# A hybrid diffusion step on one core: both filter orders, the conditioning rows and the loads of the opening stretch put in another order

## The chip, the cores and the metric

The kernel runs on one core of a Trainium2 chip. The metric is the device time of one execution in microseconds (us), lower is better. All numbers are f32.

## The reference, cut to what matters

The reference is one step of a two-layer network over 128 prompt tokens and 256 latent tokens, width 1024. Layer 0 mixes tokens with a Hyena long convolution and with grouped attention, layer 1 with latent attention; each is followed by a mixture of experts. The change touches only what comes before and inside the Hyena part of layer 0:

```python
def modulation(cond, l):
    return jax.nn.silu(cond) @ w_mod[l] + b_mod[l]          # shift, scale, gate: 6 x 1024

h = jnp.sin(fr * (z @ w1 + b1))                             # _hyena_spectrum(n, ...)
h = jnp.sin(fr * (h @ w2 + b2))
h = (h @ w3 + b3).reshape(n, HY_ORDER, 2, HY_DIM)           # 2 orders, forward and backward, 512 channels
h = h * jnp.exp(-t01[:, None] * deltas[None, :])[:, None, None, :]
h_fwd, h_bwd = h[:, :, 0], h[:, :, 1]
filt2n = jnp.concatenate([h_fwd, zeros, h_bwd[:0:-1]], axis=0)
filt2n = filt2n * lax.rsqrt(jnp.sum(filt2n * filt2n, axis=0, keepdims=True) + EPS)
return jnp.fft.rfft(filt2n, axis=0)

def _hyena(u, conv_w, conv_b, spec, bias):
    v, x1, x2 = jnp.split(_short_conv3(u, conv_w, conv_b), 3, axis=-1)
    z = x1 * long_conv(v, spec[:, 0], bias[0])              # irfft(rfft(v) * spec) + bias * v
    z = x2 * long_conv(z, spec[:, 1], bias[1])
```

The input of that mixer is `_rmsnorm(x) * (1 + sc1) + sh1`, times a 1024 x 2304 matrix (`ev_w_in`): 1536 columns for the Hyena part, 768 for queries, keys and values.

## The kernel before

Each engine has a program written out by hand, and semaphores join them. There is no scheduler: an engine does its work in the order in which it is written. Tokens stand in three tiles of 128 (`t` = 0 the prompt, 1 and 2 the latent tokens).

**Weights.** SyncE (SP) sends 1 MB pieces through a ring of nine slots (`send`); TensorE reports a slot as used (`piece_used`). The first eight pieces are the shift and scale columns of layer 0 (the stage "start": four chunks of 512 columns, two pieces each), the next nine are `ev_w_in`. Between them SP loads the filter weights `w3`, the table `decay`, the bias `hybias` (broadcast to 128 rows, twice 256 KB) and the tokens `x`. GpSimd (POOL) loads small constants, and the DFT tables `dftp` and `dfts` after piece 3.

**Conditioning.** `mod_product` multiplies a chunk by the two condition vectors in 32-column products, ScalarE copies the row out (`mod_row`), stores it in HBM (`mod_rows`), and POOL loads it back transposed (`move_row`). VectorE sums and adds it (`mod_add`); then shift `modT` and scale `modA` are ready.

**Filters.** `hidden` has 64 rows and a row of ones. `filters(od)` makes, for three token tiles and both directions, the taps of order `od`: a 65-row product on TensorE, times `decay` on VectorE, then sum and difference of the directions on VectorE. ScalarE squares them, `energies(od)` sums the squares over the rows by products with ones, and `spectrum(od)` multiplies sum and difference by the DFT tables. VectorE divides by the energy and adds the bias.

**Order on TensorE.** Two small products and two sines; chunks 0 and 1 between them; `filters(0)`; chunks 2 and 3; `energies(0)`; 24 transposes of the normed tokens (`mixer_turn`); a wait for the modulated tokens; `spectrum(0)`; then `ev_w_in` in nine pieces, numbers 6, 7, 8, 0, ..., 5. `filters(1)` stands ahead of piece 7, `energies(1)` and `spectrum(1)` ahead of piece 8. After the last piece come the transposes of the convolved channels and the DFTs of the tokens. I call the nine pieces' products *the projections*. Every f32 product is two instructions in the trace.

## Time and profile before

| | |
|---|---|
| median of three runs | 930.47 us (928.52 to 930.5) |
| the profiled execution | 928.82 us, of which the span is 927.0 |
| TensorE busy | 803.5 us (87%) |
| VectorE, ScalarE, GpSimd busy | 379.2, 272.2, 108.1 us |
| moved by DMA | 220.19 MB, mean 238 GB/s |

TensorE works through nearly the whole span, so what it does, and what it waits for, is the time to look at. The opening stretch, up to about 190 us of the span, is the one that the change touches. In rows of the trace "x12" counts instructions, and a busy time that covers several runs from the first start to the last end.

### The profile page before, as it was taken

Reading aid. Unit: us, or ns where it says so; the run is one execution under the profiler, and the core shown is the slowest. Engines: PE = TensorE matmul, PEld = TensorE weight load, DVE = VectorE, ACT = ScalarE, POOL = GpSimd, SP = SyncE. Lnnn points to the kernel's source line nnn. Section 1 sums busy time; section 2 is a strip of 40 time slices with the busy share of each in tenths; the row PEclk is TensorE's granted clock in tenths of the full one; section 3 lists DMA queues with packets and bytes.
Section 4 is the critical chain, followed back from the end, with each engine's and each line's share of the span. In section 5 each row is a group of like instructions: output and inputs, shape, how many; then the busy total and the mean of one; then the engine's idle time right before and its main releaser. Section 6 shows DMA issues by size and latency. Waiting matters only on the chain.

```text
span 927.0 us, 11593 instructions
## 1 busy us (share of the span) xinstructions
PE 803.5 (87%) x4091; PEld 447.8 (48%) x4091; DVE 379.2 (41%) x848; ACT 272.2 (29%) x636; POOL 108.1 (12%) x157
## 2 busy tenths in 40 slices
PE   4779999999888996999988599888899978999860
PEld 0236665544443464555536346545554555555430
DVE  3366583265064243332212644664651432322114
ACT  1241212121451042222211536565540332222111
POOL 2300000001000003101013002212200022010120
PEclk9989999999978997899999799999989998999995
DMA  9991222259991347899997966202109388999975
GB/s 275 370 341 50 71 93 95 90 172 345 258 371 53 130 134 250 315 405 410 411 387 262 347 246 246 93 1 93 48 1 346 125 288 312 396 411 410 384 257 208
DMA packets 84561, 220.19 MB, mean 238 GB/s; under 512 B 9636, under 2 KB 19549, under 8 KB 84185
## 3 DMA queue, kind: packets, MB, share of 16 engines
q1 hardware_dynamic: 73570, 197.04, 58.9%
q0 software_dynamic: 9120, 18.75, 5.9%
q10 hardware_dynamic: 1816, 3.68, 1.1%
q8 instruction: 33, 0.54, 0.2%
q14 instruction: 22, 0.18, 0.1%
HBM read 214.77 MB, written 14.89 MB: 248 GB/s over the span
## 4 chain that ended last, share of the span: by engine, by line
PE 63%; DMA 15%; DVE 8%; ACT 4%; SPq 3%; issue 3%; DVEq 1%; POOLq 1%; POOL 0%; ACTq 0%
PE ps L923 57%; PE ps L930 4%; DMA arena<-in_moe_w_up_dram 3%; DMA ring<-in_w_mod_dram 2%; DMA h_rows<-xn 2%; PE ps L1150 2%; DMA ring<-in_moe_w_down_dram 2%; DMA xn<-y_rows 2%; SPq L643 1%; DVEq L1909 1%; DVE negmax L1962 1%; SPq L660 1%; DMA hT<-h_rows,rows_in 1%; SPq L690 1%; ACT hT L1626 1%
## 5 line engine op out<-in xcount | busy, mean ns | idle before, releaser
L923 PE MATMUL ps<-arena 128*64 128x256 f32 (+12 forms) x1164 | 237.6, 449 | 24.8 <-ACT hT L1626 5.9
L923 PEld LDWEIGHTS ps<-arena 128*64 128x64 f32 (+4 forms) x1164 | 128.6, 168 | 115.9 <-issue 71.9
L923 PE MATMUL ps<-ring,hT 128*128 128x512 f32 (+2 forms) x384 | 133.6, 507 | 4.5 <-issue 3.9
L923 PE MATMUL ps<-ring,arena 128*64 128x256 f32 (+1 forms) x784 | 111.3, 431 | 5.5 <-DMA ring<-in_moe_w_down_dram 4.2
L923 PEld LDWEIGHTS ps<-ring,hT 128*128 128x128 f32 x384 | 73.0, 192 | 62.9 <-issue 58.5
L923 PEld LDWEIGHTS ps<-ring,arena 128*64 128x64 f32 x784 | 53.9, 137 | 51.3 <-issue 28.3
L930 PE MATMUL ps<-ident,arena 128*128 128x128 f32 (+2 forms) x332 | 51.0, 293 | 17.2 <-DVE hT L1968 4.6
L1582 ACT ACTIVATE arena<-ps 128x256 f32<-128x256 f32 (+4 forms) x88 | 38.5, 454 | 85.9 <-PE ps L923 82.2
L923 PE MATMUL ps<-hT,ring 128*128 128x384 f32 x192 | 62.1, 486 | 0.0
L2294 DVE TENSOR_TENSOR arena<-arena,ps 128x128 f32<-128x128 f32 x37 | 10.6, 288 | 124.1 <-ACT arena L1688 124.1
L923 PE MATMUL ps<-ring,condT 128*32 128x512 f32 x384 | 52.7, 674 | 8.6 <-DMA ring<-in_w_mod_dram 7.9
L930 PEld LDWEIGHTS ps<-ident,arena 128*128 128x128 f32 (+2 forms) x332 | 39.4, 143 | 38.2 <-issue 15.8
L923 PEld LDWEIGHTS ps<-hT,ring 128*128 128x128 f32 x192 | 36.5, 190 | 25.2
L2297 DVE COPY arena<-ps 64x512 f32<-64x512 f32 x37 | 25.7, 694 | 42.6 <-PE ps L923 42.2
L1694 ACT ACTIVATE arena<-ps 64x512 f32<-64x512 f32 x37 | 21.8, 590 | 66.6 <-PE ps L923 61.7
L831 POOL DMA_INDIRECT y_rows<-arena,rows_in x16 | 16.0, 1001 | 166.3 <-DVE arena L2297 166.3
L923 PE MATMUL ps<-xn,arena 128*64 128x256 f32 (+2 forms) x144 | 32.8, 473 | 2.6 <-DVE hT L1990 2.4
L1688 ACT ACTIVATE arena<-ps 128x128 f32<-128x128 f32 x37 | 10.3, 278 | 81.9 <-PE ps L923 81.9
L1962 DVE TENSOR_REDUCE negmax<-ps 128x1 f32<-128x384 f32 (+1 forms) x48 | 20.8, 461 | 29.0 <-PE ps L923 28.5
L1643 ACT ACTIVATE arena<-ps,negmax 128x384 f32<-128x384 f32 (+1 forms) x48 | 24.1, 507 | 26.0 <-DVE negmax L1962 25.9
L1618 ACT ACTIVATE xn<-x 128x1024 f32<-128x1024 f32 x12 | 12.7, 1054 | 60.7 <-DVE x L2114 57.2
L923 PEld LDWEIGHTS ps<-ring,condT 128*32 128x32 f32 x384 | 10.6, 115 | 40.8 <-issue 27.4
(301 smaller groups left out, 871.7 us busy)
## 6 DMA issues: line engine op xcount, KB each, us to landing
ring<-in_w_mod_dram SPq DMA_DIRECT2D x48, 1024.0 KB, 9.4
ring<-in_moe_w_down_dram SPq DMA_DIRECT2D x22, 1024.0 KB, 16.8
ring<-in_moe_w_gate_dram SPq DMA_DIRECT2D x38, 512.0 KB, 12.9
ring<-in_moe_w_up_dram SPq DMA_DIRECT2D x38, 512.0 KB, 15.5
arena<-in_moe_w_gate_dram SPq DMA_DIRECT2D x36, 512.0 KB, 9.5
arena<-in_moe_w_up_dram SPq DMA_DIRECT2D x36, 512.0 KB, 10.9
arena<-in_moe_w_down_dram SPq DMA_DIRECT2D x15, 1024.0 KB, 13.7
ring<-in_ev_w_in_dram SPq DMA_DIRECT2D x9, 1024.0 KB, 13.3
```

The source lines that it names most:

```text
L831: pool.indirect_dma_start(y_rows, bass.IndirectOffsetOnAxis(ap=rows_in[:, NPAIR + c:NPAIR + c + 1], axis=0), ysb[:, c % 2, :], None, bound ...
L923: mm = pe.matmul(out, lhsT, rhs, **kw)
L930: mm = pe.transpose(out, src, ident[:, :])
L1150: mm = pe.transpose(ps[XT_BANKS[half]][:, q * P:(q + 1) * P], src[:, (4 * half + q) * P:(4 * half + q + 1) * P], ident[:, :])
L1582: drain_inc(act.activation(dst, src, kw.pop("func", ACT.Copy), **kw), stage, i)
L1618: act.activation(xn[:, t, :], x[:, t, :], ACT.Square, accum_out=ssq[:, s, t:t + 1]).then_inc(squares, 1)
L1643: drain_inc(act.activation(mprobs[:, i % 2, r, 0:nk], bank_of(f"mS{g}", u)[:, 0:nk], ACT.Exp, bias=negmax[:, c:c + 1], accum_out=psumexp[: ...
L1688: act.activation(sil[:, e % 2, :], ps[GU_BANKS[e % 2]][:, 0:P], ACT.Silu).then_inc(silu_ready[l], 1)
L1694: act.activation(dst, ps[Y_BANKS[e % 2]][0:HALF, :], ACT.Copy).then_inc(done[l], 1)
L1962: dve.tensor_reduce(negmax[:, c:c + 1], bank[:, 0:nk], AXX, ALU.max, negate=True).then_inc(negmax_ready, 1)
L2294: dve.tensor_tensor(mid[:, e % 2, :], sil[:, e % 2, :], ps[GU_BANKS[e % 2]][:, P:2 * P], ALU.mult).then_inc(mid_ready[l], 1)
L2297: dve.tensor_copy(dst, ps[Y_BANKS[e % 2]][HALF:P, :]).then_inc(y_read[1][l], 1)
```

## The change

1. SP loads the filter inputs first (they were on ScalarE's queue), then the condition vectors. `hybias` is 4 KB, no broadcast. The DFT tables go from POOL's queue to SP's, ahead of piece 4. Most small constants of POOL wait for piece 5.
2. The filter weights are padded: rows 65 to 127 of `w3` and `hidden` are zero, and products have 128 rows. GpSimd forms the sum and the half difference of the forward and backward weights once (`wsum`, `w3`), so TensorE gives sum and difference directly.
3. `filters`, `energies` and `spectrum` of both orders stand ahead of the projections. The energy division leaves the spectrum: the root of the energy is turned (`root_turn`), inverted, and folded into the short convolution's coefficients (`conv_scaled`); the bias becomes an addition to the first tap (`bias_taps`).
4. The four "start" rows are not stored and loaded back: eight 2-column products turn each (`mod_turn`).
5. 10 and 8 products of ones with ones (`warm`) stand ahead of the first two products. Energies are 32 rows wide instead of 128.

```diff
     B.stage("filt1", 1)
+    B.stage("filt2", 1)
     mod_stage("start", 0)
-    B.stage("filt2", 1)
+    B.stage("filt3.0", 2 * NT)
+    B.stage("modT0", 1)
+    B.stage("filt3.1", 2 * NT)
     mod_stage("start", 1)
...
+                    load(sp, in_filt, zT, d["zT"])
+                    load(sp, in_filt, filtc[0:EMB, 3 + HID:3 + 2 * HID], d["ev_filt_w1"][0])
...
                 if i == 2:
+                    sp.wait_ge(w3_ready, 1)
                     load(sp, in_filt3, w3[0:HID, :, :], d["ev_filt_w3"][0].rearrange("k (a b) -> k a b", b=HY))
                     load(sp, in_filt3, w3[HID:HID + 1, :, :], d["ev_filt_b3"].rearrange("k (a b) -> k a b", b=HY))
+                    load(sp, in_filt3, decay, d["decay"].rearrange("p (a b) -> p a b", b=HY))
+                    load(sp, in_filt3, hybias[0:1, :, :], d["ev_hy_bias"])
                 if i == 4:
...
+                    load(sp, in_spec, dftp, d["dft_p"].rearrange("p (a b) -> p a b", b=NPR))
+                    load(sp, in_spec, dfts, d["dft_s"].rearrange("p (a b c) -> p a b c", b=2, c=NSA))
...
+            loaded(pool, in_filt3)
+            pool.tensor_tensor(wsum, w3[:, 0::2, :], w3[:, 1::2, :], ALU.add)
+            pool.drain()
+            pool.tensor_tensor(w3[:, 1::2, :], w3[:, 0::2, :], w3[:, 1::2, :], ALU.subtract)
+            pool.drain().then_inc(w3_ready, 1)
...
-            for i in range(len(CHUNKS["start"])):
-                move_row("start", i)
...
+            def mod_turn(i):
+                l, v, half = CHUNKS["start"][i]
+                row = modrow_of("start", i)
+                bank = claim(f"modT{i}")
+                drained_wait(pe, f"mod{l}.{v}.{half}")
+                for j in range(KT):
+                    mm = product(bank[64 * half:64 * half + 64, 2 * j:2 * j + 2], row[:, j::KT], rowsel[:, :, 0], carries=False, start=True, stop=True)
+                fill_inc(mm, f"modT{i}")
...
+                        split = w3[:, 2 * od + 1, :] if r else wsum[:, od, :]
+                        mm = product(bank[:, :], hidden[:, t * P:(t + 1) * P], split, carries=False, start=True, stop=True)
...
+                for t, r in ((0, 0), (1, 0), (0, 1), (1, 1), (2, 0), (2, 1)):
+                    pe.wait_ge(esq_ready, od * (NT + 1) + max(t, 1) + 2)
+                    g = GRP[t]
+                    mm = product(bank[32 * g:32 * g + 32, :], onesm[:, 0:32], sqs[:, t, r, :], start=t < 2 and r == 0, stop=t != 1 and r == 1)
...
             for q in (6, 7, 8, 0, 1, 2, 3, 4, 5):
-                if q == 7:
-                    filters(1)
-                if q == 8:
-                    energies(1)
-                    spectrum(1)
-                if q == 0:
-                    pe.wait_ge(spec_done, 12)
...
             def filter_squares(od, t):
-                act.wait_ge(sum_ready, od * NT + t + 1)
+                act.wait_ge(tile_ready, od * NT + t + 1)
                 if od:
-                    filled_wait(act, "energy0", min(t, 1))
-                act.activation(filt[:, t, 0, :], sqd, ACT.Copy)
-                act.activation(sqs[:, t, 0, :], sqd, ACT.Square)
-                act.activation(sqs[:, t, 1, :], filt[:, t, 1, :], ACT.Square)
+                    filled_wait(act, "energy0")
+                for r in range(2):
+                    act.activation(sqs[:, t, r, :], filt[od][:, t, r, :], ACT.Square)
                 act.drain().then_inc(esq_ready, 1)
```

TensorE in the opening stretch, before: from `filters(0)` to the first piece of the queries, `filters(1)`, and the last of the 65-row products. "ring,condT" are conditioning chunks, "arena,gb" energies, "ident,xn" the transposes of the normed tokens, "ring,hT" projections of a piece.

```order
L923 MATMUL ps<-arena 128x512 x6
L923 MATMUL ps<-ring,condT 32x512 x16
L923 MATMUL ps<-arena,gb 128x512 x6
L930 MATMUL ps<-ident,xn 128x128 x24
L923 MATMUL ps<-arena 128x512 x10
L1366 MATMUL ps<-ident,arena 128x48
L923 MATMUL ps<-ring,hT 128x256 x24
L923 MATMUL ps<-arena 128x512 x6
L923 MATMUL ps<-ring,hT 128x256 x24
L923 MATMUL ps<-arena,gb 128x512 x6
L923 MATMUL ps<-arena 128x512 x10
L923 MATMUL ps<-ring,hT 128x256 x24
```

And in the change, from `energies(1)` on ("rowsel" marks `mod_turn`, 128x32 the turned roots):

```order
L949 MATMUL ps<-arena,gb 32x512 x6
L949 MATMUL ps<-rowsel,modrow 64x2 x8
L1385 MATMUL ps<-ident,arena 128x32 x8
L949 MATMUL ps<-ring,condT 32x512 x8
L1422 MATMUL ps<-ident,arena 128x48
L949 MATMUL ps<-rowsel,hT 64x2 x8
L956 MATMUL ps<-ident,xn 128x128 x24
L949 MATMUL ps<-arena 128x512 x5
L1385 MATMUL ps<-ident,arena 128x32 x8
L949 MATMUL ps<-arena 128x512 x10
L949 MATMUL ps<-ring,hT 128x256 x72
L949 MATMUL ps<-hT,ring 128x384 x96
```

The 22 filter products that stood between the projections' first pieces are gone from there, and 15 of the 20 spectrum products stand between the turned tokens and the projections.

ScalarE, before, from the third chunk's row to the modulation (L1618 and L1620 are the norm of the tokens, L1582 the copy of a row, L1626 the modulation):

```order
L1582 ACTIVATE modrow<-ps 128x512
L1609 DMA mod_rows<-modrow 8x512
L1790 ACTIVATE arena<-gb 128x512
L1791 ACTIVATE arena<-gb 128x512
L1792 ACTIVATE arena<-arena 128x512
L1582 ACTIVATE hT<-ps 128x512
L1609 DMA mod_rows<-hT 8x512
L1618 ACTIVATE xn,ssq<-x 128x1024
L1620 ACT_TABLE_LOAD
L1620 ACTIVATE ssq<-ssq 128x1
```

The same stretch in the change (L1857 is the root of an energy, L1851 the squares, L1672 and L1674 the norm, L1634 the copies):

```order
L1857 ACT_TABLE_LOAD
L1857 ACTIVATE arena<-ps,gb 32x512 x2
L1851 ACTIVATE arena<-arena 128x512 x6
L1634 ACTIVATE modrow<-ps 128x512
L1672 ACTIVATE xn,ssq<-x 128x1024
L1674 ACTIVATE ssq<-ssq 128x1
...
L1634 ACTIVATE hT<-ps 128x512
L1857 ACTIVATE arena<-ps,gb 32x512 x2
L1680 ACTIVATE hT<-ps,modT,modA 128x128 x12
```

The squares of order 1 now stand behind the roots of order 0, and the copy of the last chunk's row stands behind the norm of all three token tiles, where it stood ahead of it.

## Rows read from the trace of the kernel before

**Rows 1.** The page: the span and the instructions.

```profile
span 927.0 us, 11593 instructions
```

**Rows 2.** The chain that ended last, 0 to 220 us: start, duration, what.

```profile
24.32 20.73 DMA ring<-in_w_mod_dram
...
45.10 1.98 PE ps L923 x8
...
47.81 5.30 DMA mod_rows<-hT
...
53.40 6.24 DMA hT<-mod_rows
...
185.74 2.62 PE ps L930 x24
```

**Rows 3.** Windows: busy us of each engine, granted clock, DMA share, GB/s.

```profile
25.00:45.00 20.00, 15.55 (x36) 4.15 (x34) 8.82 (x14) 5.60 (x10) 5.81 (x11) 1.00 1.04 370
```

**Rows 4.** TensorE in order of time, 52 to 130 us: start, duration, what.

```profile
62.41 11.06 PE L923 MATMUL ps<-arena 128*128 128x512 f32 x20 [5.92 <-ACT hT L1626]
...
73.59 10.63 PE L923 MATMUL ps<-ring,hT 128*128 128x256 f32 x48
84.05 5.32 PE L923 MATMUL ps<-arena 65*128 65x512 f32 x12
89.20 10.52 PE L923 MATMUL ps<-ring,hT 128*128 128x256 f32 x48
99.57 5.31 PE L923 MATMUL ps<-arena,gb 128*128 128x512 f32 x12
104.72 8.75 PE L923 MATMUL ps<-arena 128*128 128x512 f32 x20
113.30 10.52 PE L923 MATMUL ps<-ring,hT 128*128 128x256 f32 x48
123.66 6.61 PE L923 MATMUL ps<-hT,ring 128*128 128x384 f32 x20
```

**Rows 5.** TensorE in order of time, 0 to 60 us.

```profile
13.36 1.94 PE L923 MATMUL ps<-ring,condT 128*32 128x512 f32 x8 [0.90 <-DMA ring<-in_w_mod_dram]
...
18.54 1.94 PE L923 MATMUL ps<-ring,condT 128*32 128x512 f32 x8 [1.74 <-DMA ring<-in_w_mod_dram]
...
24.43 10.61 PE L923 MATMUL ps<-arena 65*128 65x512 f32 x12 [1.32 <-DMA gb<-in_ev_hy_bias_dram]
...
46.96 6.84 PE L923 MATMUL ps<-arena,gb 128*128 128x512 f32 x12
53.63 2.85 PE L930 MATMUL ps<-ident,xn 128*128 128x128 f32 x24
```

**Rows 6.** Windows of TensorE alone: busy, granted clock, DMA share, GB/s.

```profile
24.40:35.10 10.70, 10.67 (x16) 1.00 1.06 359
...
62.40:66.80 4.40, 4.39 (x5) 0.50 1.11 349
```

**Rows 7.** All engines, 0 to 70 us: loads issued at the start.

```profile
0.73 0.62 ACTq L643 DMA_DIRECT2D arena<-in_zT_dram  x1
...
1.67 0.98 SPq L660 DMA_DIRECT2D ring<-in_w_mod_dram  x2
```

**Rows 8.** GpSimd by line and shape.

```profile
L889 POOL TENSOR_TENSOR arena<-arena,statA 128x1152 f32<-128x1152 f32 x4 | 8.5, 2114 | 79.8 <-DVE statA L2069 79.8
```

**Rows 9.** TensorE, 196 to 260 us: conditioning chunks later on.

```profile
197.30 3.64 PE L923 MATMUL ps<-ring,condT 128*32 128x512 f32 x32
```

**Rows 10.** TensorE, 326 to 345 us: products of 16 columns.

```profile
337.00 1.86 PE L923 MATMUL ps<-routw,hT 128*128 128x16 f32 x16
```

**Rows 11.** ScalarE by line and shape, 0 to 70 us.

```profile
L1618 ACT ACTIVATE xn<-x 128x1024 f32<-128x1024 f32 x3 | 3.1, 1046 | 0.6 <-ACT hT L1582 0.6
...
L1791 ACT ACTIVATE arena<-gb 128x512 f32<-128x512 f32 x3 | 1.8, 613 | 0.0
...
L1620 ACT ACT_TABLE_LOAD x1 | 1.3, 1283 | 0.0
```

More of the change, by code:

```diff
@@ L80 @@
 }
-MOVED = [chunk for where in CHUNKS for chunk in CHUNKS[where] if chunk[1] not in (G1, G2)]
+MOVED = [chunk for where in CHUNKS if where != "start" for chunk in CHUNKS[where] if chunk[1] not in (G1, G2)]
 MODA_ORDER = [(0, 0), (0, 1), (1, 0), (1, 1)]
@@ L1342, in _, with warm @@
+            def warm(bank, n):
+                for _ in range(n):
+                    pe.matmul(bank[:, 0:P], onesm, onesm, start=True, stop=True)
+            pe.wait_ge(ones_set, 1)
+            bank = claim("filt1")
+            warm(bank, WARM_FIRST)
             loaded(pe, in_filt)
-            bank = claim("filt1")
             mm = product(bank[0:HID, 0:T], filtc[0:EMB, 3 + HID:3 + 2 * HID], zT, start=True, stop=True)
             fill_inc(mm, "filt1")
-            mod_step("start", 0)
+            bank = claim("filt2")
@@ L1347, in _ @@
+            warm(bank, WARM_SIN)
             loaded(pe, in_filt2)
             pe.wait_ge(sin_done, 1)
[L1349 removed]
             mm = product(bank[0:HID, 0:T], filtc[:, 3:3 + HID], hidden[0:HID, :], carries=False, start=True, stop=True)
             fill_inc(mm, "filt2")
[L1352 to L1358 removed]
@@ L1359, in _ @@
-            energies(0)
-            loaded(pe, in_mod)
-            for t in range(NT):
-                mixer_turn(0, t)
+            mod_step("start", 0)
+            pe.wait_ge(w3_ready, 2)
+            pe.wait_ge(sin_done, 2)
+            filters(0)
+            mod_turn(0)
+            filters(1)
+            mod_step("start", 1)
+            loaded(pe, in_spec)
+            spectrum(0, 1)
+            energies(0)
+            mod_turn(1)
+            mod_step("start", 2)
+            energies(1)
@@ L1363, in _ @@
+            mod_turn(2)
+            root_turn(0)
+            mod_step("start", 3)
             loaded(pe, in_dft)
-            spectrum(0)
             bank = claim("convT")
@@ L1367, in _ @@
             fill_inc(mm, "convT")
+            mod_turn(3)
+            for t in range(NT):
+                mixer_turn(0, t)
+            spectrum(1, 1)
+            root_turn(1)
+            spectrum(0, 0)
+            spectrum(1, 0)
             for i in range(6):
@@ L1600, in mod_row @@
                         act.wait_ge(mod_out[sent % 2], 16 * (sent // 2 + 1))
-                    if v in (G1, G2):
+                    if where == "start" and i >= 2:
+                        filled_wait(act, f"modT{i - 2}")
+                    if where == "start" or v in (G1, G2):
                         copy_out(name, 0, row, bank_of(name)[:, :])
@@ L1802, in heads_copy @@
                     copy_out(f"qkv{q}", t, qkv[:, t, q * 256:(q + 1) * 256], bank_of(f"qkv{q}", t)[:, 0:256])
+            mod_step("start", 0)
+            first_rows(0)
             for t in range(NT):
                 filter_squares(0, t)
-                if t:
-                    mod_step("start", t + 1)
+            first_rows(1)
+            mod_step("start", 1)
+            energy_roots(0)
+            for t in range(NT):
+                filter_squares(1, t)
+            mod_step("start", 2)
             loaded(act, in_x)
@@ L1920, in mod_step @@
                 rows = slice(64 * half, 64 * half + 64)
-                total = (moved_rows[where][:, 128:144] if where == "start" else row_total)[rows].rearrange("p (j c) -> p j c", c=2)
+                total = row_total[rows].rearrange("p (j c) -> p j c", c=2)
                 dve.wait_ge(mod_moved[n % 2], 16 * (n // 2 + 1))
@@ L1926, in mod_step, with mod_add, mod_scale @@
                 dve.tensor_tensor(modT[rows, l, v, :, :], total, modT[rows, l, v, :, :], ALU.add)
+                mod_scale(l, v, half)
+            def mod_add(i):
+                l, v, half = CHUNKS["start"][i]
+                rows = slice(64 * half, 64 * half + 64)
+                bank = filled_wait(dve, f"modT{i}")
+                turned = bank[rows, 0:2 * KT].rearrange("p (j c) -> p j c", c=2)
+                drain_inc(dve.tensor_tensor(modT[rows, l, v, :, :], turned, modT[rows, l, v, :, :], ALU.add), f"modT{i}")
+                mod_scale(l, v, half)
+            def mod_scale(l, v, half):
                 if half == 0 or v in (SH1, SH2):
@@ L2444, in _ @@
+            filters(0)
+            mod_add(0)
+            filters(1)
+            imaginary_copies(0)
+            bias_taps(0)
+            mod_add(1)
+            mod_add(2)
+            root_inverse(0)
             norm(0)
-            energies(0)
-            for i in range(1, 5):
-                mod_step("start", i)
+            bank = filled_wait(dve, "convT")
+            drain_inc(dve.tensor_copy(convT[:, :, :], bank[:, 0:48].rearrange("p (a b) -> p a b", b=3 * NCH)), "convT")
+            mod_add(3)
```

252 lines of the change are left out of this document (137 added, 115 removed).

## The prediction

> **What bounds the kernel now.** I began with the page and the chain of work that ended last, then read TensorE in order of time. The span is 927.0 us [rows 1]. On the chain, a weight piece is the first long entry: it lands at 45.1, TensorE multiplies it for 2.0 us, and then the row goes out to HBM (5.3) and comes back (6.2) [rows 2]. TensorE meanwhile runs out of work: 5.92 us idle, and it starts the first spectrum only at 62.41, once the tokens are modulated [rows 4]. From there to 185.74, where the transposes behind the projections begin [rows 2], it has no gap that a row shows. In this second part a microsecond of TensorE's work is a microsecond of the span; in the first part it is DMA that sets the pace: its share is 1.04 and it moves 370 GB/s from 25 to 45 us [rows 3], while a filter's products wait for a load before they start at 24.43 [rows 5].
>
> The projections themselves take, start to next start, 10.46 (73.59 to 84.05), 10.37 (89.20 to 99.57), 10.36 (113.30 to 123.66) and 62.08 us (123.66 to 185.74): 93.3 us [rows 2, 4]. Were nothing else between them, they would have to start at 185.74 - 93.3 = 92.5 us for the end that they have now. The other 30 us from 62.4 on are `spectrum(0)` 11.2 (with a small transpose), `filters(1)` 5.15, `energies(1)` 5.15 and `spectrum(1)` 8.6 [rows 4]. So the question of this change is one number: when do the projections start, if all of the filter work is ahead of them? Call it S. The gain is 92.5 - S. What follows the projections is the same work, and its loads are released by it: ring slots by pieces used, the first expert weights by the second inverse DFT. I let all of it move as one block.
>
> **TensorE's clock.** The same 128x512 instruction takes two lengths. 12 of them from 84.05 take 5.15 us, 0.43 each [rows 4]; 12 from 24.43 take 10.6, 0.88 each [rows 5]. From 62.4 to 66.8, five take 4.39, again 0.88, and the granted clock there is 0.50, that is 1.2 instead of 2.4 GHz [rows 6]. At 24.4 the column says 1.00 [rows 6]; there I go by the length, and call it slow too. The slow filter products had 65 rows and stayed slow for all of 10.6 us; the 128-row energies from 46.96 take 6.84 for 12, which is slow ones for about 3 us and fast ones after; the spectra from 62.41 turned fast after 4.4 us [rows 5, 6]. The padded products have 128 rows. I take it that the first 4 of them are slow and what follows is fast.
>
> **When the filters start.** Four more small loads stand ahead of the first weight pieces on SP. The longest of them is issued in 0.62 us, and the pieces' issue began at 1.67 [rows 7], so the delay is up to 2.5 us; DMA begins with little in its queues, so I take 1.5. TensorE took up the second piece at 13.36 and the third at 18.54, with 1.5 MB (`w3` and a piece) between them: 5.2 us [rows 5]. Now `w3` and `decay`, 1.25 MB, come right after the second: 13.4 + 1.5 + 4.3 = 19.2. Then GpSimd adds and subtracts 1024 columns each. The nearest row is 2.11 us for 1152 columns [rows 8]: 1.9 each, 3.8 in all. The filters start at 23, where they now start at 24.4; the two sines are done by then, and the `warm` products are hidden behind the same wait. The Trainium skill (GPSIMD Engine Reference, 3.1 on elementwise work) speaks against giving this work to GpSimd: it gives 4.5 us for 2048 columns where VectorE takes half. By it the filters would start 0.7 us later, an estimate from that page; no run here has shown this very operation.
>
> **TensorE's work from there to S.** `filters(0)`: 4 slow and 8 fast instructions, 3.5 + 3.4 = 7.0. `filters(1)`: 5.2. Four half spectra of 10 instructions: 17.2. Three conditioning chunks: two take 3.64 when fast [rows 9], so 1.8 each, 5.5. That row also shows that 32-column products at different columns run side by side: 32 instructions at 0.11 each, a quarter of 0.43. The new energies are 32 wide in two places: 8 instructions pairwise and 4 alone, 8 x 0.43 = 3.5 each, 7.0 for both, where they took 5.2 each. `mod_turn`: the nearest row is 16 instructions of 16 columns in 1.7 us (337.00 to the next start; 1.86 with the tail) [rows 10]; its weights are half as wide, so 0.8 is the other end. I take 1.3, four times 5.2. Two `root_turn`s of 8 transposes at 0.12 each (24 take 2.85 [rows 5]): 1.9. The 24 transposes of the tokens 2.8, the convolution's 0.2. Sum: 52.0 us.
>
> **Stalls in it.** Two, both by ScalarE's order. (a) The squares of order 1 stand behind the root of order 0. The first energy ends at about 45.3; then a table load of 1.28, two roots and six squares of 0.61 each [rows 11], with drains: the last squares are ready at 51.5, those that `energies(1)` needs first at 50.3. TensorE, after a turn and a chunk (3.1), is there at 48.5. It loses 1.8. (b) The last chunk's row is copied only after the norm of all three tiles, and VectorE takes up the norm only after the turned roots, at 56.5. Three squares of 1.05 [rows 11] in turn with small steps of VectorE take 4 us or so, then 0.6 for the copy: 60.9. TensorE is there at 58.4: 2.5 us lost. Behind that nothing is late: the half spectrum of order 1 covers the modulation (12 instructions each on ScalarE and VectorE), and the remaining ones cover its copies. Together 4.3, and 0.5 for banks.
>
> S = 23 + 52.0 + 4.8 = 79.8, and the gain 92.5 - 79.8 = 12.7 us. Against the profiled execution's 928.8 us that is 916.1. The median of the runs, 930.5, stands 1.7 above that execution; I put the changed kernel's median between, at **917 us**.
>
> **What costs nothing, and its cover.** The removed store and reload (11.5 us with the sums behind them) are worth nothing beyond this sum: they are on the path before, but S is set by TensorE's work. DMA: the eight conditioning pieces, filters, tables and tokens are 12 MB, at 370 GB/s [rows 3] some 34 us, so the last chunk is there well ahead of 56; all of `ev_w_in` by about 66, ahead of S. If that cover were gone, each us late is a us. The small constants that POOL now loads after piece 5 (six ahead of the convolution's transpose, at some 0.6 of issue each as `zT` [rows 7]) land around 47, some 10 us early. The two scaled copies per channel tile on ScalarE add under 0.7 us to a tile that TensorE takes 62.08 / 12 = 5.2 us for.
>
> **Rivals.**
> *The zero rows do not count* (0.13). The padded filter products stay at 0.88, as the 65-row ones did. For it: 10.6 us of slow products that nothing sped up. Against: the instruction now names 128 rows, and those did speed up. Then 20 instructions cost 0.45 more, 9 us: S near 88.8, 925 to 926 us.
> *TensorE's order is tighter than I count* (0.15). `mod_turn` at 0.8, the clock already fast when the filters start, weights there 2 us earlier and no stall (b): 2 + 1.8 + 2 + 2.5 = 8 us less: 908.
> *The clock never holds in the opening* (0.06). This one ends slower. Chunks, turns of 2 columns and short waits come between all the wide products, and if they let the clock fall, the 48 us that I count as fast take up to twice as long. It decides at 12.7 us: if more than a quarter of that work runs slow, the gain is gone; if all of it does, S is 128 and the kernel at 960; half of it gives 940. Before, a chunk between wide products at 197.3 stays fast [rows 9], which speaks against. The Trainium skill (TensorE: Matmul & The Clock Gate, Part 4 on transposes) says that transposes do not count as busy for the clock; by it the 24 token transposes behind stall (b) would let it fall, and the half spectrum after them would run slow for its 10 instructions, some 4 us by the two lengths. In the rows, 24 transposes from 53.63 end with the fall, but a wait of 5.92 us stands between [rows 4, 5], so they don't decide it.
> *Nothing gained* (0.02): the opening ends where it did, because a load (`in_dft` or `x`) takes the place of the old wait at some 12 us later than I have it.
>
> **How the numbers follow.** My forecast, 911 to 922, has 0.64. With the tighter order to 908 and the zero-row case to 925 the range is 907 to 925, and leaves out the clock that never holds. A measurement of this kernel can tell about 0.2%, 1.9 us, from no change. Faster: all of the first three but the edge, 0.91; same 0.02; slower 0.07, which is the third rival and a load that I have not seen.
>
> **What would show it.** Filters start at 22 to 25 us, and their instructions fall from 0.88 to 0.43 within the first five; the second energies wait 2 us for ScalarE squares; `mod_turn` of the last chunk waits 2 to 3 us for the row's copy; the first "ring,hT" product starts at 77 to 83 and the transposes behind the projections 93 us later; from there to the end the two traces keep one distance. Wrong would be: the weights' sum on GpSimd taking twice its row, a granted clock of 0.50 between 45 and 80 us, or a distance that shrinks once the expert weights bind.

## The result, and the profile after

The changed kernel took 924.44 us (median of 20 runs, 916.4 to 930.17), the kernel before 929.31 us (20 runs in turn with it, 923.75 to 937.78). The ratio is 0.994, with a 95% interval of 0.9914 to 0.9967: faster by about 5.6 us, not by 12.7. (The two medians stand 4.9 us apart; the ratio is taken over the runs in the fast state alone, and one of the 20, at 930.17, was not in it.) The time is inside the range given, at its upper edge, and outside the narrower forecast of 911 to 922.

The profiled execution of after took 929.42 us, longer than its own median. So I read stages by where they stand in the span, not by the span.

```profile
span 927.6 us, 11800 instructions
...
PE 815.1 (88%) x4207; PEld 464.2 (50%) x4207; DVE 354.3 (38%) x822; ACT 278.6 (30%) x648; POOL 111.1 (12%) x155
```

TensorE is busy for 11.6 us more than before (work and slower clock together: the mean granted clock of this trace is 0.929, before's 0.947) and VectorE for 25 us less. TensorE in order of time, the opening (start, duration, what, and in brackets the idle time before it and who ended it):

```profile
23.05 7.98 PE L949 MATMUL ps<-arena 128*128 128x512 f32 x12 [6.81 <-POOLq L796]
30.96 2.08 PE L949 MATMUL ps<-rowsel,modrow 128*64 128x2 f32 x16
32.97 5.42 PE L949 MATMUL ps<-arena 128*128 128x512 f32 x12
38.31 1.92 PE L949 MATMUL ps<-ring,condT 128*32 128x512 f32 x16
40.17 4.56 PE L949 MATMUL ps<-arena 128*128 128x512 f32 x10
44.66 3.63 PE L949 MATMUL ps<-arena,gb 128*32 128x512 f32 x12
48.22 2.08 PE L949 MATMUL ps<-rowsel,hT 128*64 128x2 f32 x16
50.23 1.92 PE L949 MATMUL ps<-ring,condT 128*32 128x512 f32 x16
52.48 3.63 PE L949 MATMUL ps<-arena,gb 128*32 128x512 f32 x12 [0.33 <-ACTq L1852]
56.04 2.08 PE L949 MATMUL ps<-rowsel,modrow 128*64 128x2 f32 x16
58.05 0.68 PE L1385 MATMUL ps<-ident,arena 32*128 32x32 f32 x8
58.66 3.41 PE L949 MATMUL ps<-ring,condT 128*32 128x512 f32 x16
...
62.92 2.05 PE L949 MATMUL ps<-rowsel,hT 128*64 128x2 f32 x16 [0.58 <-ACT hT L1634]
64.90 4.57 PE L956 MATMUL ps<-ident,xn 128*128 128x128 f32 x24
69.31 4.46 PE L949 MATMUL ps<-arena 128*128 128x512 f32 x10
...
82.99 31.24 PE L949 MATMUL ps<-ring,hT 128*128 128x256 f32 x144
...
175.99 2.78 PE L956 MATMUL ps<-ident,arena 128*128 128x128 f32 x24
```

Most rows have their counterpart in [rows 4, 5]. Filters start at 23.05, where 24.43 stood, behind a wait of 6.81 us for GpSimd; the wait of 5.92 us for the tokens is gone; the projections start at 83.0, where 92.5 was their equivalent before; the transposes behind them stand at 175.99, 9.6 us ahead of before's, which this view puts at 185.58 (the 185.74 of [rows 2] is the chain's figure; the chain of after has 176.15). The rows with 128x2 are the turned conditioning rows, 2.0 us for 16.

Now the same view further on, where the change touches only the list of stages, and adds one wait of VectorE for copies of the spectra that were made long before:

```profile
203.63 8.85 PE L949 MATMUL ps<-xn,arena 128*128 128x512 f32 x20
215.27 5.34 PE L949 MATMUL ps<-ring,condT 128*32 128x512 f32 x32 [2.78 <-DVE arena L2606]
221.49 8.93 PE L949 MATMUL ps<-arena 128*128 128x128 f32 x48 [0.89 <-ACT arena L1634]
```

and the same piece of before, with the transposes behind the projections as its first row:

```profile
185.58 2.78 PE L930 MATMUL ps<-ident,arena 128*128 128x128 f32 x24
...
213.22 8.85 PE L923 MATMUL ps<-xn,arena 128*128 128x512 f32 x20
222.01 3.64 PE L923 MATMUL ps<-ring,condT 128*32 128x512 f32 x32
226.23 8.96 PE L923 MATMUL ps<-arena 128*128 128x128 f32 x48 [0.59 <-DVE arena L2512]
```

Up to 203.63 after leads by 9.6 us. Then it waits 2.78 us for VectorE, the conditioning chunk takes 5.34 us instead of 3.64, and at the second inverse DFT the lead is 226.23 - 221.49 = 4.7 us. Half of what the opening won is given back here. VectorE's row for that moment shows the releaser, an instruction that reads a PSUM bank and ends at 215.2:

```profile
214.53 0.68 DVE L2606 TENSOR_TENSOR arena<-ps,arena 128x512 f32<-128x512 f32 x1
```

**Who meets whom.** The eight PSUM banks are given out by one list. A stage without banks of its own takes the next ones in turn:

```python
    def stage(self, name, count, banks=None):
        out = []
        for i in range(count):
            if banks is None:
                b = self.turn
                self.turn = (self.turn + 1) % 8
```

The chunks of the later conditioning (`mod_stage("gqa", i, BANK_M)`) have fixed banks, 6 and 7 by turns. The change adds four turned rows and two root turns to the list, takes two energy results off it, and so moves `self.turn` by 4 for all that follows. Worked out from the list, the second forward DFT (`fwd1`, six results) had banks 5, 6, 7, 0, 1, 2 and now has 1, 2, 3, 4, 5, 6. The chunk behind it takes bank 6. Before, that was the second of six results, long read; now it is the last, and the chunk waits until VectorE's product at L2606 has read it. This was a theory (A) until the first two experiments.

### The profile page after: what moved, and what is told of

It reads as the page before. It is cut to its first block, busy times and chain, and to the rows that moved or that the text cites. A ratio compares the mean times of both kernels' runs of the same rounds, so it can differ in the third digit from the quotient of the medians.

```text
span 927.6 us, 11800 instructions
## 1 busy us (share of the span) xinstructions
PE 815.1 (88%) x4207; PEld 464.2 (50%) x4207; DVE 354.3 (38%) x822; ACT 278.6 (30%) x648; POOL 111.1 (12%) x155
## 4 chain that ended last, share of the span: by engine, by line
PE 69%; DMA 10%; DVE 7%; ACT 4%; issue 4%; DVEq 1%; SPq 1%; POOLq 1%; ACTq 0%; POOL 0%
PE ps L949 61%; DMA arena<-in_moe_w_up_dram 5%; PE ps L956 5%; PE ps L1186 2%; DVEq L1983 1%; DMA h_rows<-xn 1%; DMA xn<-y_rows 1%; DMA hT<-h_rows,rows_in 1%; SPq L703 1%; DMA hT<-h_rows,row_now 1%; DVE xn L2445 1%; DVE negmax L2047 1%; DMA mod_rows<-modrow 1%; PE ps L1200 1%; ACT arena L1634 1%
## 5 line engine op out<-in xcount | busy, mean ns | idle before, releaser
L949 PE MATMUL ps<-arena 128*64 128x256 f32 (+11 forms) x1164 | 236.6, 448 | 23.6 <-POOLq L796 6.8
L949 PEld LDWEIGHTS ps<-arena 128*64 128x64 f32 (+3 forms) x1164 | 128.5, 168 | 112.8 <-issue 65.2
L1634 ACT ACTIVATE arena<-ps 128x256 f32<-128x256 f32 (+4 forms) x94 | 42.2, 463 | 89.2 <-PE ps L949 85.6
L2379 DVE TENSOR_TENSOR arena<-arena,ps 128x128 f32<-128x128 f32 x37 | 10.7, 288 | 124.8 <-ACT arena L1742 124.8
L949 PE MATMUL ps<-ring,condT 128*32 128x512 f32 x384 | 50.3, 655 | 2.8 <-DVE arena L2606 2.8
L1742 ACT ACTIVATE arena<-ps 128x128 f32<-128x128 f32 x37 | 10.2, 277 | 82.3 <-PE ps L949 82.3
L1672 ACT ACTIVATE xn<-x 128x1024 f32<-128x1024 f32 x12 | 12.7, 1055 | 60.1 <-DVE x L2199 57.2
L1186 PE MATMUL ps<-ident,hT 128*128 128x128 f32 x136 | 20.0, 294 | 11.5 <-DMA hT<-h_rows,rows_in 8.6
```

Source lines behind the costliest of these rows:

```text
L949: mm = pe.matmul(out, lhsT, rhs, **kw)
L1186: mm = pe.transpose(ps[XT_BANKS[half]][:, q * P:(q + 1) * P], src[:, (4 * half + q) * P:(4 * half + q + 1) * P], ident[:, :])
L1634: drain_inc(act.activation(dst, src, kw.pop("func", ACT.Copy), **kw), stage, i)
L1672: act.activation(xn[:, t, :], x[:, t, :], ACT.Square, accum_out=ssq[:, s, t:t + 1]).then_inc(squares, 1)
L1742: act.activation(sil[:, e % 2, :], ps[GU_BANKS[e % 2]][:, 0:P], ACT.Silu).then_inc(silu_ready[l], 1)
L2379: dve.tensor_tensor(mid[:, e % 2, :], sil[:, e % 2, :], ps[GU_BANKS[e % 2]][:, P:2 * P], ALU.mult).then_inc(mid_ready[l], 1)
```

## The experiments

All in five rounds beside the kernel before. The table sets two measures side by side: how far the second inverse DFT stands ahead of before's 226.23 in the one profiled execution, and what the whole kernel gained (one minus the ratio, of 930 us; the interval is the ratio's). One profile is one execution: with the same loads, the filters start anywhere from 22.09 (e4) to 23.61 (e5) in these traces, so I read no difference of less than about 1.5 us in one start alone as an effect, and go by rows next to each other.

```
                     median    ratio [95%]              ahead at the   whole kernel
                     us                                 inverse DFT    gained, us
after                924.44    0.994  [0.9914, 0.9967]      4.7          5.6
e1_banks             917.57    0.9876 [0.9841, 0.9911]      9.1         11.5
e2_clash             932.78    1.0035 [1.0012, 1.0058]     -5.1         -3.3
e3_no_warm           924.21    0.9928 [0.9897, 0.996]       5.5          6.7
e4_65rows            933.84    1.0033 [1.0005, 1.0061]     -3.8         -3.1
e5_row_trip          934.36    1.007  [1.0038, 1.0103]    -10.3         -6.5
e6_turn_only         921.04    0.9914 [0.9885, 0.9943]      4.1          8.0
e7_free_banks        929.08    0.9992 [0.9962, 1.0022]      2.3          0.7
e8_wide_between      923.11    0.9916 [0.9881, 0.9952]      7.9          7.8
e9_turn_early        920.36    0.9871 [0.9825, 0.9916]      9.4         12.0
e10_turn_twice       921.79    0.9907 [0.9874, 0.994]       7.7          8.6
e11_row_trip2        922.5     0.9936 [0.991, 0.9963]       6.4          6.0
e12_norm_early       918.12    0.9857 [0.9818, 0.9896]     10.2         13.3
```

### e1_banks: the changed kernel with the bank order of before

```diff
     B.stage("uT", 3 * NCH)
+    B.turn = (B.turn + 4) % 8
     B.stage("vtok", NT)
```

> The changed kernel with the turn of the PSUM banks moved on by four ahead of the transposes of the convolved channels, so that the DFTs, inverse DFTs and conditioning chunks meet on the banks that they had before the change. Theory A (the shifted turn of the banks makes the chunk after the second forward DFT wait for VectorE): the 2.8 us of idle ahead of its 32 instructions and their 5.3 us go back to none and 3.6; the first transposes of the attention stand 9 to 10 us ahead of the kernel before instead of 5; 3 to 5 us less than the changed kernel. Theory B (the wait comes from VectorE or from the clock, whatever the bank): the wait and the distance of 5 us stay.

Measured: 917.57 us, 0.9876. TensorE:

```profile
212.85 3.64 PE L950 MATMUL ps<-ring,condT 128*32 128x512 f32 x32
217.09 8.96 PE L950 MATMUL ps<-arena 128*128 128x128 f32 x48 [0.60 <-DVE arena L2610]
```

The wait is gone and the chunk takes 3.64 again; the intervals of e1 and after just miss each other (0.9911 and 0.9914). Theory A holds.

### e2_clash: the same line in the kernel before

```diff
     B.stage("uT", 3 * NCH)
+    B.turn = (B.turn + 4) % 8
     B.stage("vtok", NT)
```

> The kernel before with the same move of the bank turn, which gives it the banks that the changed kernel has in the DFTs. Theory A: the wait of 2.5 to 3 us behind the second forward DFT appears in the old kernel, its chunk takes up to 5.3 us instead of 3.6, and the kernel takes 3 to 5 us more. Theory B: nothing moves by more than 0.5 us there.

Measured: 932.78 us, 1.0035, as theory A has it. The wait is now in before, with the same number:

```profile
225.43 4.98 PE L924 MATMUL ps<-ring,condT 128*32 128x512 f32 x32 [2.78 <-DVE arena L2510]
231.31 8.93 PE L924 MATMUL ps<-arena 128*128 128x128 f32 x48 [0.90 <-ACT arena L1583]
```

One line puts the clash in and takes it out, in either kernel, without any of the rest of the change. Of its 4.5 us here and 4.9 in after, 2.8 are the wait, 1.3 to 1.7 the chunk behind it, whose instructions run slow again after the wait, and the rest the later copy (0.90 for 0.60).

### e3_no_warm: without the products that only keep TensorE busy

Left out: the products of ones at the start, whose results nothing uses.

```diff
-WARM_FIRST, WARM_SIN = 10, 8
+WARM_FIRST, WARM_SIN = 0, 0
```

> The changed kernel without the 18 products of ones ahead of the first two filter products. Theory A (the filters' speed is set by what runs from their own start): filters start at 23, 5 to 6 of their instructions at 0.85 us, projections at 83 as in the changed kernel, within 1 us. Theory B (the products of ones carry the fast clock into the filters): the filter products, chunk 0 and turn 0 run slow for longer, the projections start 2 to 5 us later. The two small products may each take 0.7 us longer in both, ahead of the wait for the weights.

Measured: 924.21 us, 0.9928, which the runs can't tell from after. Theory A holds. Filters:

```profile
22.23 7.98 PE L949 MATMUL ps<-arena 128*128 128x512 f32 x12 [6.09 <-POOLq L796]
```

They take 7.98 us with warm products and without; 6 us of waiting stand between the warm products and them. They won nothing in the opening.

### e4_65rows: the filter products over 65 rows, as before

```diff
-                        split = w3[:, 2 * od + 1, :] if r else wsum[:, od, :]
-                        mm = product(bank[:, :], hidden[:, t * P:(t + 1) * P], split, carries=False, start=True, stop=True)
+                        split = w3[0:HID + 1, 2 * od + 1, :] if r else wsum[0:HID + 1, od, :]
+                        mm = product(bank[:, :], hidden[0:HID + 1, t * P:(t + 1) * P], split, carries=False, start=True, stop=True)
```

> The changed kernel with filter products of 65 rows instead of 128 zero-padded ones (the weights stay padded in memory, the result is the same). Theory A (the padded rows are what lets the clock rise): all 24 filter instructions at 0.85 to 0.88 us, the two sets take 10.5 each instead of 7.9 and 5.3, projections start 6 to 9 us later than at 83, at 89 to 92. Theory B (rows do not matter, the clock rises by length of work): 7.9 and 5.3 as with 128 rows, projections at 83.

Measured: 933.84 us, 1.0033.

```profile
22.09 10.61 PE L949 MATMUL ps<-arena 65*128 65x512 f32 x12 [5.75 <-POOLq L796]
...
34.64 10.61 PE L949 MATMUL ps<-arena 65*128 65x512 f32 x12
```

Both filters run at 0.88 an instruction to the end, and the granted clock reads 0.50 from 22 to 46 us, where the padded ones took 7.9 and 5.3. The projections start at 91.5, 8.5 us later, as theory A has it. So the rows of zeros pay for nearly the whole opening: with 65 rows the transposes behind the projections stand at 184.49, only 1.1 us ahead of before's, and the bank clash, which this kernel has too, takes more than that. The second filter matters most: before, it stood between projections and ran fast with 65 rows (5.15, [rows 4]); ahead of them it stays slow. What the 65 rows do is keep it slow, not make it slow.

### e6_turn_only: before, with the rows turned by TensorE and nothing else

```diff
+            def mod_turn(i):
...
+                for j in range(KT):
+                    mm = product(bank[64 * half:64 * half + 64, 2 * j:2 * j + 2], row[:, j::KT], rowsel[:, :, 0], carries=False, start=True, stop=True)
...
             filters(0)
-            for i in (2, 3, 4):
-                mod_step("start", i)
-            energies(0)
             loaded(pe, in_mod)
+            mod_turn(0)
+            mod_turn(1)
+            mod_step("start", 2)
+            mod_step("start", 3)
+            mod_turn(2)
+            energies(0)
+            mod_turn(3)
```

The bank order behind `uT` is kept as before. The cut leaves out VectorE's side, where `mod_add` takes the place of the sums.

> The kernel before with only the conditioning rows turned by TensorE; filters, energies, loads and bank turn of the later stages as before the change. Theory A (the filter work ahead of the projections fills TensorE's slow and idle time, the turn alone fills little): the first spectrum starts at 58 to 60 instead of 62.4, the 5.9 us of idle shrink to 2 or less, the transposes behind the projections stand 3 to 6 us earlier. Theory B (the trip through HBM is the whole gain): they stand 9 us earlier, as in the changed kernel.

Measured: 921.04 us, 0.9914.

```profile
56.21 4.54 PE L933 MATMUL ps<-ident,xn 128*128 128x128 f32 x24
60.55 8.82 PE L926 MATMUL ps<-arena 128*128 128x512 f32 x20
```

The wait of 5.92 us and the trip are gone; the spectrum starts 1.9 us sooner and runs fast from its first instruction (8.82 for 11.06). The lead at the transposes behind the projections is 4.2 us, less than half of after's 9.6: theory A, not B. The whole kernel gained 8.0 us (5.3 to 10.7), more than this lead; that part is open, see below. As it stands, the turned rows alone do no worse than the whole change with its clash.

### e7_free_banks: before, with the first spectrum's banks free earlier

```diff
-    B.stage("spec0", 2 * NT)
+    B.stage("spec0", 2 * NT, (6, 7, 4, 5, 0, 1))
+    B.turn = (B.turn + 6) % 8
```

> The kernel before with one list changed: the first spectrum's first two banks are the two that the turned tokens do not hold. Theory A (in the idle 5.9 us TensorE waits for banks, not for data): two spectrum banks, 8 instructions, run in the idle time, the transposes behind the projections stand 3 to 5 us earlier. Theory B (it waits for the modulated tokens or for the DFT tables): nothing moves.

Measured: 929.08 us, 0.9992: no change that can be told.

```profile
55.22 3.60 PE L924 MATMUL ps<-arena 128*128 128x512 f32 x8
63.03 8.09 PE L924 MATMUL ps<-arena 128*128 128x512 f32 x12 [4.21 <-ACT hT L1627]
```

Eight spectrum products did move into the idle time, so part of the 5.92 us was a wait for banks and not for tokens. The other 12 still wait for ScalarE's modulated tiles, which depend on the trip of the row, and start at 63. The lead is 2.3 us, under theory A's 3 to 5, and the runs don't show it. Free banks alone do not replace the change.

### e5_row_trip: e1, with the rows going through HBM again

```diff
             filters(0)
-            mod_turn(0)
             filters(1)
```

and so for all four rows; `move_row` on GpSimd and the sums on VectorE come back, where the new adds stood.

> The changed kernel with the banks mended, and the four opening conditioning rows go through HBM again as before the change (16 small products a row leave TensorE). Theory A (in the new order TensorE's own work sets the start of the projections, and the four turns are 8 us of it): TensorE finishes its share about 6 us earlier, the last row lands some 13 us after its copy, and the two nearly cancel: projections at 81 to 85, within 2 us of 83.4. Theory B (the trip is what the change removes, as the chain of before says): the modulated tokens come 10 us later and so do the projections, at 91 or more, and most of the gain is gone.

Measured: 934.36 us, 1.007; projections at 102.7.

```profile
49.68 7.10 PE L952 MATMUL ps<-arena 128*128 128x512 f32 x10 [11.71 <-DVE arena L2498]
```

Worse than any theory said, and for a reason of my own making: VectorE has the first row's sum ahead of its work on the second filter, and the row comes back late (VectorE takes it up at 48.4), since GpSimd loads its constants first and issues the row's load only at 42.4. All waited behind it. It does not measure the trip.

### e11_row_trip2: the same, with VectorE's sums behind the filter work

```diff
             filters(0)
-            mod_step("start", 1)
             filters(1)
...
-            mod_step("start", 4)
+            for i in range(1, 5):
+                mod_step("start", i)
             for t in range(NT):
```

> As e5_row_trip, but VectorE adds the four rows only when all filter work ahead of them is done, so that nothing else waits behind a row's trip through HBM. Theory A (the trip hides behind 15 half-spectrum products, and four turns cost TensorE 8 us): projections at 81 to 86. Theory B (the last row lands 12 to 13 us after its copy and the spectra cannot run meanwhile, since they need the banks of the turned tokens): projections at 88 to 93, TensorE idle for 6 to 12 us ahead of the half spectra.

Measured: 922.5 us, 0.9936; projections at 86.1.

```profile
56.18 1.16 PE L959 MATMUL ps<-ident,xn 128*128 128x128 f32 x8
60.62 2.00 PE L959 MATMUL ps<-ident,xn 128*128 128x128 f32 x16 [3.28 <-ACT arena L1854]
62.46 1.88 PE L952 MATMUL ps<-arena 128*128 128x512 f32 x4
72.19 4.72 PE L952 MATMUL ps<-arena 128*128 128x512 f32 x6 [7.84 <-ACT hT L1677]
```

Without the 64 narrow products TensorE is through with the transposes at 62.5, and they run fast (24 in 3.2 us). Then it waits 7.84 us for the tokens. That is theory B's wait, but the start lies at theory A's edge, between the two ranges. Net, the trip costs 86.1 - 83.4 = 2.7 us against e1: the turn wins a wait of 7.84 and pays 8.0 us of narrow products and the slow stretch behind them, of which much filled other waits.

### e10_turn_twice: e1, with the last row's 16 products made twice

```diff
-                for j in range(KT):
+                for j in list(range(KT)) * (2 if i == 3 else 1):
```

> The changed kernel with the banks mended, and the last turn's 16 products done twice into the same place. Theory A: the projections start 2 us later for the products themselves, and up to 2 us more since more of the 24 transposes behind it run slow (0.21 instead of 0.115 us each): 85.4 to 87.5. Theory B (the 24 transposes are slow by themselves, whatever stands ahead of them): exactly 2.0 later, at 85.4 to 85.6, with the transposes as slow as before.

Measured: 921.79 us, 0.9907; projections at 84.8, 1.4 later than in e1.

```profile
62.01 3.97 PE L950 MATMUL ps<-rowsel,hT 128*64 128x2 f32 x32 [0.69 <-ACT hT L1635]
65.91 5.38 PE L957 MATMUL ps<-ident,xn 128*128 128x128 f32 x24
71.09 4.51 PE L950 MATMUL ps<-arena 128*128 128x512 f32 x10
```

A turn of 16 costs 2.0 us (3.97 for 32). The transposes behind take 5.38 us (e1: 5.27; before: 2.85 [rows 5]), and the spectrum behind them is fast, 0.45 an instruction. The start is below both ranges, because the last turn itself began 0.6 us sooner than in e1 (62.01 for 62.65). The run does not decide between the theories: in e1 the transposes were slow from first to last already (granted clock 0.50 from 62 to 69 us), so a longer turn could not slow them further.

### e8_wide_between: e1, with ten wide products between the narrow ones

`spectrum(0, 0)` is moved from behind the transposes to ahead of the last chunk, its copies on ScalarE and its three banks in the list with it.

```diff
             root_turn(0)
+            spectrum(0, 0)
             mod_step("start", 3)
...
             root_turn(1)
-            spectrum(0, 0)
```

> The changed kernel with the banks mended, and the real half spectrum of order 0 (10 instructions of 512 columns) moved ahead of the last conditioning chunk, between the narrow products. Theory A (the slow stretch from 58.5 to 69 comes of a run of narrow products and transposes, and stalls on ScalarE): the last chunk falls from 2.8 to 1.9, the 24 transposes from 5.1 to 2.8, the stall of 1.1 goes, projections start at 79 to 81 instead of 83.4 and the kernel takes 2 to 4 us less. Theory B (the slow stretch is by position in time or transposes never hold the clock): it stays with the transposes, projections at 82 to 84.

Measured: 923.11 us, 0.9916; projections at 84.6, 1.2 later than in e1.

```profile
57.69 5.98 PE L950 MATMUL ps<-arena 128*128 128x512 f32 x10
63.60 1.92 PE L950 MATMUL ps<-ring,condT 128*32 128x512 f32 x16
...
68.98 2.08 PE L950 MATMUL ps<-rowsel,hT 128*64 128x2 f32 x16 [3.27 <-ACT arena L1858]
70.99 4.41 PE L957 MATMUL ps<-ident,xn 128*128 128x128 f32 x24
```

and on ScalarE:

```profile
67.57 1.35 ACT L1858 ACTIVATE arena<-ps,gb 32x512 f32<-32x512 f32 x2
```

The chunk is fast, but the wide products in front of it pay (5.98 for 4.46), and the transposes are slow all the same. The last turn waits 3.27 us, and most of that is a clash of the kind of e1 and e2: the move shifts the list by three, the last turn gets bank 7, and the second energy still lies there until ScalarE has taken its root (the row above, done at 68.92). The row that the turn needs was copied at 66.25. So some 2.7 us of the start at 84.6 are the clash, and this run does not show whether wide work in between would win.

### e9_turn_early: e1, with the first row turned while TensorE waits for weights

```diff
             mod_step("start", 0)
+            mod_turn(0)
             pe.wait_ge(w3_ready, 2)
...
             filters(0)
-            mod_turn(0)
             filters(1)
```

The bank of the turned row moves ahead of the filters' in the list.

> The changed kernel with the banks mended, and the first turn of a conditioning row (16 products of 2 columns) moved from behind the first filters into the 6.6 us in which TensorE waits for the filter weights. Theory A (a turn costs its 2.0 us of TensorE and in some places a slow stretch behind it): the projections start 2 to 4 us earlier than at 83.4, at 79 to 81.5. Theory B (TensorE's order is not what sets the start; ScalarE and VectorE chains are): they start within 0.5 us of 83.4.

Measured: 920.36 us, 0.9871; projections at 83.2.

```profile
18.82 2.08 PE L950 MATMUL ps<-rowsel,modrow 128*64 128x2 f32 x16 [3.12 <-ACT modrow L1635]
...
33.21 4.56 PE L950 MATMUL ps<-arena 128*128 128x512 f32 x10 [1.22 <-DVE modT L2009]
...
62.17 2.05 PE L950 MATMUL ps<-rowsel,hT 128*64 128x2 f32 x16 [2.01 <-ACT hT L1635]
```

Two us of work moved into a wait, and S gained 0.2: theory B. The wait ahead of the last turn, for ScalarE's copy of the row, grew from 1.06 in e1 to 2.01, and a wait of 1.22 appeared at the second filter, for the bank that holds the turned row until VectorE has added it. The chain of ScalarE and VectorE (squares, roots, norm, copy of the last row) sets when the last turn can start, so what TensorE saves ahead of it turns into waiting.

### e12_norm_early: e9, with VectorE's norm moved forward

```diff
             mod_add(1)
+            norm(0)
             mod_add(2)
             root_inverse(0)
-            norm(0)
```

> As e9_turn_early, and VectorE does the norm of the tokens ahead of the third row's addition and of the inverse root, so that ScalarE is free when the last chunk is done. Theory A: the stall of 1.1 us ahead of the last turn goes too, and a shorter idle time leaves less slow clock: projections at 77.5 to 80.5, 12 to 15 us ahead of the 92.5 of the kernel before, and the kernel 13 to 17 us under the kernel before. Theory B (the norm was not what held the last row): as e9_turn_early.

Measured: 918.12 us, 0.9857; projections at 82.3.

```profile
61.49 2.05 PE L950 MATMUL ps<-rowsel,hT 128*64 128x2 f32 x16 [0.58 <-ACT hT L1635]
```

The wait falls to 0.58, so VectorE's norm was part of what held the row. S is another 0.9 lower, far from theory A's 77.5 to 80.5. e1, e9 and e12 beat the kernel before, e1 and e12 the changed one too; the intervals of the three overlap, so which is best stays open.

## Why the prediction was right and where it failed

The forecast gain was 12.7 us. The opening gained 9.6, because S came out at 83.0 and not at 79.8; 4.9 of that were given back behind the projections, and 4.7 were left at the second inverse DFT. The whole kernel gained 5.6, less than half of the forecast. That the time still lies in the range is luck: the upper bound of 925 was set for zero rows that do not count, and they do count.

**The step that failed most** is "what follows the projections is the same work ... I let all of it move as one block". The work is the same, the banks are not. The prediction counted bank waits in the opening (0.5 us) and did not read the list for the stages behind it. It cost 4.9 us of the 9.6 (shown by e1 and e2). The sign that the prediction named for being right, "from there to the end the two traces keep one distance", failed here.

**The start.** Filters start at 23.05, forecast 23. That is right by two errors: the loads were there at 17.9, not 19.2, and GpSimd took more, 4.7 us and a gap:

```profile
17.94 2.34 POOL L793 TENSOR_TENSOR arena<-arena 128x1024 f32<-128x1024 f32 x1 [12.71 <-DMA gb<-in_ev_hy_bias_dram]
20.60 2.34 POOL L795 TENSOR_TENSOR arena<-arena 128x1024 f32<-128x1024 f32 x1 [0.33 <-issue]
```

I took 3.8 from a row of another shape [rows 8]. The Trainium skill (GPSIMD Engine Reference, 3.1 on elementwise work) gives 4.5 for 2048 columns; the trace has 4.68, in two instructions of 1024.

**TensorE's work**, forecast 52.0, measured 59.0 (from each start to the next in the rows above). `mod_turn` is the largest term: 2.0 instead of 1.3, four times, 2.8 us. It was mis-sized beyond its bounds of 0.8 to 1.7: 128x2 products take longer an instruction (0.126) than the 16-column products that I took as a guide (0.106). The last chunk took 3.34 instead of 1.8 and the 24 transposes 4.4 instead of 2.8, together 3.1 us of slow clock: a granted clock of 0.50 between 45 and 80 us, which the prediction named as a sign of being wrong. `filters(0)` took 7.9 (7.0: by the two lengths six slow instructions, not four), `filters(1)` 5.3 (5.2), the half spectra 17.6 (17.2), the energies 7.1 (7.0), the root turns 1.2 (1.9).

**The stalls**, forecast 4.8, measured 0.33 + 0.58 = 0.9. Both were placed rightly (the rows behind ScalarE's squares, and ahead of the last turn) and sized for a TensorE that comes sooner. Stall (b): TensorE was expected at 58.4 and came at 62.3. ScalarE was later too (the row was copied at 62.8, not 60.9), but TensorE's own slower work had filled most of the wait, as e9 shows from the other side, where TensorE came sooner and the wait grew to 2.01. S = 83.0 for 79.8: 7.0 more work, 3.9 less stall.

**The rivals.** The zero rows do count (7.9 and 5.3 for 10.6; e4). Of "TensorE's order is tighter" only the small stall came; the turns took more, not less. "The clock never holds" is wrong as a whole: half spectra, energies and the second filter ran at the fast length. (Its price was also a little off: 48 us more on S = 79.8 give some 965, not 960.) But a part of it is true: chunk and transposes around the last two turns ran slow, and the record shows it there:

```profile
59.00:62.00 3.00, 3.00 (x17) 0.50 1.11 349
65.00:69.00 4.00, 4.00 (x23) 0.60 1.02 307
```

(windows of TensorE: busy, granted clock, DMA share, GB/s; 0.50 is 1.2 of 2.4 GHz.) Products of 2 columns stood just ahead. For the 24 transposes the traces agree: in each of the nine kernels in which a turn of 16 stands right ahead of them they take 4.4 to 5.4 us, and in e10 the granted clock falls at about 64.4, while TensorE does nothing but such products; in before, e2, e7 and e11, with no turn ahead, they take 2.9 to 3.2 (in e5 they are slow too, behind a wait of 6.16 us). Elsewhere they don't: behind the second turn the chunk takes 1.92 in every kernel with the order of after. Behind the first turn the second filter takes 5.42 in after and 7.12 in e1, whose granted clock is 0.53 from 32 to 34 us:

```profile
31.12 7.12 PE L950 MATMUL ps<-arena 128*128 128x512 f32 x12
```

And the last chunk, behind a turn and the turned roots, took 3.41 in after and 2.81 in e1, which have the same order there, and 1.92 in e9 and 2.97 in e12, which have one order too. That narrow products let the clock fall is what these rows fit; when they do and when not, the runs do not show. The rule weighed in the prediction (TensorE: Matmul & The Clock Gate, Part 4 on transposes, of the Trainium skill: they do not count as busy) would have the half spectrum behind the transposes slow, some 4 us. The trace disagrees: its 10 took 4.46, and 4.51 in e10, where all that ran since the 2-column products was 24 transposes. They did not keep the clock from rising.

**What stays open.** From the first experts on the code is the same in all the kernels, and yet the stretch from the first experts to the start of latent attention took 178 to 184 us in the 14 traces, and from there to the last product 376 to 386. After's profile has 184.0 and 383.8, before's 182.8 and 379.6: this is why the profiled spans are equal though the opening is 4.7 us ahead. Kernels with the bank turn of before and with that of after lie on both sides, so I have no reason to put it to the change; nor have I found what makes it. In all lines of the table but two (e5 and e6) the lead lies within the interval of what the whole kernel gained; e6 gained 8.0 where its lead was 4.1, and there the surplus is of this unexplained kind (its stretch took 178.1). For the same reason the 5.6 us of the result can be read as 4.7 of lead plus what the runs scatter, but not proved to a microsecond. Not run: the padded rows alone in the kernel before, and e8 with its bank clash taken out.

## What to carry to other kernels

When stages are added to or removed from a plan that deals out banks in turn, write down, for every stage behind the edit that has a fixed bank, who had that bank last, before and after; a clash there costs a wait and the slow stretch behind it, and one line takes it out (e8 ran into one as well). A contraction padded to 128 rows with zeros can be worth far more than it seems (8.5 us here for 24 instructions) where the work starts at the slow clock, as it did here behind a wait. Work that goes to an engine in products of 2 columns is priced by the instruction (0.126 us with 2 columns, 0.106 with 16), not by the columns, and the engine's next work should be priced at both clock lengths.

## What the runs showed of the hardware

- Products over 65 rows stayed at 0.88 us an instruction for two runs of 12 (10.61 us each), products over 128 rows, in the same place and of the same width, fell to 0.44 within the first run of 12 (7.98, then 5.42; in e1 6.88, then, behind 16 products of 2 columns, 7.12).
- 12 energies of 32 output columns, written side by side, took 3.63 us where the full width took 5.31 [rows 4].
- Products of ones ahead of a wait of 6 us changed nothing behind it (7.98 with and without).
- GpSimd took 2.34 us for a 128x1024 sum of f32; it took 2.11 for 128x1152 in another place [rows 8].
